# Two-head attention rounds in another order: PE weighs the values of three pairs back first, then scores, then transposes

## The reference

```python
def global_axial_attention(q, k, v, gq, gk):        # "A": 8 heads of 64, 2 key/value heads
    ...
        s = jnp.einsum('bqkgd,bskd->bkgqs', qi, k).astype(jnp.float32)
        p = jax.nn.softmax(s, axis=-1)
        return jnp.einsum('bkgqs,bskd->bqkgd', p.astype(v.dtype), v)
...
def neighbourhood_attention(q, k, v, rpb):           # "C": 8 heads of 64, a window of columns, a bias
    ...
        s = s + bias.astype(jnp.float32)[None]
        p = jax.nn.softmax(s.reshape(B, C_HEADS, GRID_W, win_r * NA_COLS), axis=-1)
        return jnp.einsum('bhqrj,brqjhd->bqhd', p, v_nb)
```

## Time and profile before

| | us |
|---|---|
| median of 3 runs | 3302.02 |
| lowest, highest | 3294.03, 3302.18 |
| the profiled execution | 3301.9 |
| its span, first to last instruction | 3300.1 |
| PE busy in the span | 3174.4 (96%) |
| DVE, ACT, POOL busy | 1688.9, 1196.6, 145.8 |
| mean granted TensorE clock | 0.989 |

### The profile page before, as it was taken

How to read it: one execution, slowest core, us unless ns; L and a number is a source line. 1 busy time by engine, 2 the same in 40 slices (tenths; PEclk the granted TensorE clock), 3 DMA queues, 4 the chain that set the end, 5 groups by cost and what they waited for, 6 DMA issues and landing times.

```text
span 3300.1 us, 42252 instructions
## 1 busy us (share of the span) xinstructions
PE 3174.4 (96%) x17113; PEld 2612.7 (79%) x17113; DVE 1688.9 (51%) x2230; ACT 1196.6 (36%) x1612; POOL 145.8 (4%) x203
## 2 busy tenths in 40 slices
PE   8899999999989899999999889999999999999999
PEld 7667888888867588888887568888888888788887
DVE  3565446553444644565527855552543434555543
ACT  3544235343333622444323244342321222344432
POOL 2030000000011200000002110000000000000000
PEclk9999999999989999999999999999999999999999
DMA  6112323322422032233322113323221121223222
GB/s 170 49 39 77 101 90 102 102 83 97 110 68 74 27 102 91 101 102 97 100 96 78 53 58 102 102 83 108 92 89 64 64 90 64 75 85 101 89 89 89
DMA packets 229781, 285.02 MB, mean 86 GB/s; under 512 B 5156, under 2 KB 188492, under 8 KB 229388
## 3 DMA queue, kind: packets, MB, share of 16 engines
q1 hardware_dynamic: 225628, 266.89, 24.8%
q0 software_dynamic: 4016, 16.16, 2.0%
HBM read 280.93 MB, written 2.10 MB: 86 GB/s over the span
## 4 chain that ended last, share of the span: by engine, by line
PE 87%; DVE 10%; ACT 2%; issue 1%; POOL 0%; DMA 0%; DVEq 0%; POOLq 0%; ACTq 0%
PE ps L1595 19%; PE ps L1597 18%; PE ps L1596 18%; PE ps L1710 6%; PE ps L1709 6%; PE ps L1708 6%; DVE t_wlo L1045 2%; ACT t_whi L674 1%; PE ps L1634 1%; PE ps L1633 1%; PE ps L1632 1%; PE ps L1802 1%; DVE t_vb L1514 1%; PE ps L1981 1%; PE ps L2160 1%
## 5 line engine op out<-in xcount | busy, mean ns | idle before, releaser
L1045 DVE TENSOR_TENSOR t_wlo<-t_wraw,t_whi 128x2048 fp32r<-128x2048 f32 x252 | 583.1, 2314 | 1302.7 <-ACT t_whi L674 1302.7
L1595 PE MATMUL ps<-t_hh,t_whi 128*128 128x512 f32 (+1 forms) x2704 | 1012.0, 374 | 10.8 <-DVE t_accv L1241 5.1
L1596 PE MATMUL ps<-t_hl,t_whi 128*128 128x512 f32 (+1 forms) x2704 | 1002.6, 371 | 0.0
L1597 PE MATMUL ps<-t_hh,t_wlo 128*128 128x512 f32 (+1 forms) x2704 | 1002.5, 371 | 0.0
L674 ACT ACTIVATE t_whi<-t_wraw 128x2048 fp32r<-128x2048 f32 x252 | 482.8, 1916 | 1374.4 <-PE ps L1597 954.0
L1595 PEld LDWEIGHTS ps<-t_hh,t_whi 128*128 128x128 f32 x2704 | 510.6, 189 | 113.2 <-issue 14.9
L1596 PEld LDWEIGHTS ps<-t_hl,t_whi 128*128 128x128 f32 x2704 | 510.6, 189 | 88.3 <-issue 2.4
L1597 PEld LDWEIGHTS ps<-t_hh,t_wlo 128*128 128x128 f32 x2704 | 510.4, 189 | 87.8
L1708 PE MATMUL ps<-t_whi,t_midh 128*128 128x512 f32 x704 | 274.4, 390 | 0.0
L1710 PE MATMUL ps<-t_whi,t_midl 128*128 128x512 f32 x704 | 274.0, 389 | 0.0
L1709 PE MATMUL ps<-t_wlo,t_midh 128*128 128x512 f32 x704 | 273.9, 389 | 0.0
(11 more groups left out here) (275 smaller groups left out, 3749.8 us busy)
## 6 DMA issues: line engine op xcount, KB each, us to landing
t_wraw<-in_w_in_dram SPq DMA_DIRECT2D x46, 1024.0 KB, 5.3
t_wraw<-in_w_up_dram SPq DMA_DIRECT2D x44, 1024.0 KB, 5.1
t_wraw<-in_ffn_w_in_dram SPq DMA_DIRECT2D x44, 1024.0 KB, 5.1
t_wraw<-in_w_kv_dram SPq DMA_DIRECT2D x24, 1024.0 KB, 5.1
t_wraw<-in_w_down_dram SPq DMA_DIRECT2D x20, 1024.0 KB, 5.0
t_wraw<-in_ffn_w_out_dram SPq DMA_DIRECT2D x20, 1024.0 KB, 5.0
t_wraw<-in_w_branch_dram SPq DMA_DIRECT2D x12, 1024.0 KB, 5.0
t_wraw<-in_w_q_dram SPq DMA_DIRECT2D x12, 1024.0 KB, 5.1
```

The costliest lines, as they stand in the source:

```text
L1045: v.tensor_tensor(wlo[slot][:, :], wraw[slot][:, :], whi[slot][:, :].bitcast(F32), ALU.subtract).then_inc(w_lo, 1)
L1595: te.matmul(out, wh, xh, start=first, stop=False)
L1596: te.matmul(out, wh, xl, start=False, stop=False)
L1597: return te.matmul(out, wl, xh, start=False, stop=last)
```

## The change

On all engines the rounds are written in one new order. In round j:

- PE: weigh pair j-3, scores of pair j, (pooling matmul), transposes of both heads of pair j-2. Scores of pair j wait for the exponentials of pair j-2 in A and in C.
- ACT: exponentials of pair j-1, (pooling, `y_round`), copies of both heads of pair j-2.
- DVE: maxima of pair j, divide both heads of pair j-1, (`y_rest`).

Scores of pair 1 now stand ahead of the last `row_tile` of the stage before. In C the maxima write the sums back into the PSUM bank of the scores, and the exponentials read them there, so the wait for `turned` moves from DVE's maxima to ACT's exponentials. `pA` gets a fourth slot. The two tiles at the end are split: one ahead of the last transposes, one behind them, and the last weighing comes after both, in A too. The split of a weight chunk and the pooling steps on ACT and DVE stand in other rounds. In A the banks of the scores are swapped.

```diff
-POOL_PAIRS = (3, 7, 11, 15)
 SLOTS = 3
+PAIR_SLOTS = 4
...
-                pA = sb("pA", SLOTS * T, stack=u)
+                pA = sb("pA", PAIR_SLOTS * T, stack=u)
...
-        def score_bank(n):
-
-            return bank(6 * (n // 2 % 2) + n % 2)
+        def score_bank(kind, n):
+
+            return bank(6 * ((n // 2 + (kind == "A")) % 2) + n % 2)
...
-                slots = 4 if kind == "C" else SLOTS
+                per = 2 if kind == "C" else 4
+                pairs = 4 * per
 
                 def exp(n):
                     g = n0 + n
-                    s, q = g % slots, g % 4
+                    s, q = g % PAIR_SLOTS, g % 4
                     act.wait_ge(maxed, g + 1)
-                    if kind == "A" and n >= slots:
-                        act.wait_ge(turned, g - slots + 1)
+                    if n >= PAIR_SLOTS:
+                        act.wait_ge(turned, g - PAIR_SLOTS + 1)
+                    p, scores = pbuf[:, s * T:(s + 1) * T], score_bank(kind, n)
                     if kind == "C":
                         for i in range(2):
-                            p = pbuf[:, s * T + i * WIN:s * T + (i + 1) * WIN]
-                            ins = sc.activation(p, p, ACT.Exp, bias=small[:, 2 * q + i:2 * q + i + 1], scale=-1.0,
+                            ins = sc.activation(p[:, i * WIN:(i + 1) * WIN], scores[:, i * WIN:(i + 1) * WIN], ACT.Exp,
+                                                bias=small[:, 2 * q + i:2 * q + i + 1], scale=-1.0,
                                                 accum_out=small[:, 8 + 2 * q + i:9 + 2 * q + i])
                     else:
-                        ins = sc.activation(pbuf[:, s * T:(s + 1) * T], score_bank(n), ACT.Exp, bias=small[:, q:q + 1],
-                                            scale=rq[:, n:n + 1], accum_out=small[:, 8 + q:9 + q])
+                        ins = sc.activation(p, scores, ACT.Exp, bias=small[:, q:q + 1], scale=rq[:, n:n + 1],
+                                            accum_out=small[:, 8 + q:9 + q])
                     ins.then_inc(probs, 1)
...
-                exp(0)
-                exp(1)
-                if 0 in extra:
-                    extra[0]()
-                per = 2 if kind == "C" else 4
-                pairs = 4 * per
-                for j in range(pairs + 2):
-                    if 1 <= j <= pairs:
-                        copy(2 * j - 1)
-                    if j > per and (j - 1) % per == 0:
-                        y_round(n0, (j - 1) // per - 1, per, kind)
-                    if j < pairs:
-                        copy(2 * j)
-                    if j < pairs - 1:
-                        exp(2 * j + 2)
-                        exp(2 * j + 3)
-                    if j and j in extra:
+                for j in range(1, pairs + 4):
+                    if j <= pairs:
+                        exp(2 * j - 2)
+                        exp(2 * j - 1)
+                    if j in extra:
                         extra[j]()
+                    if j >= per + 3 and (j - 3) % per == 0:
+                        y_round(n0, (j - 3) // per - 1, per, kind)
+                    if 2 <= j < pairs + 2:
+                        copy(2 * j - 4)
+                        copy(2 * j - 3)
...
-                pair_maxima(n0, 0, scores_in, factors)
-                divide(n0, pbuf, T)
-                for j in range(pairs + 2):
+                for j in range(pairs + 4):
+                    if j in extra:
+                        extra[j]()
                     if j < pairs:
-                        divide(n0 + 2 * j + 1, pbuf, T)
-                    if j == 0:
-                        if j in extra:
-                            extra[j]()
-                        pair_maxima(n0, 1, scores_in, factors)
-                    if j < pairs - 2:
-                        pair_maxima(n0, j + 2, scores_in, factors)
-                    if j < pairs - 1:
-                        divide(n0 + 2 * j + 2, pbuf, T)
-                    if j and j in extra:
-                        extra[j]()
-                    if j > per and (j - 1) % per == 0:
-                        pair_out((j - 1) // per - 1)
+                        pair_maxima(n0, j, scores_in, factors)
+                    if 1 <= j <= pairs:
+                        divide(n0 + 2 * j - 2, pbuf, T)
+                        divide(n0 + 2 * j - 1, pbuf, T)
+                    if j >= per + 3 and (j - 3) % per == 0:
+                        pair_out((j - 3) // per - 1)
...
-                def scores_c(n, s, q, l=l):
+                def scores_c(n, q, l=l):
                     hp, bb = divmod(n // 2, 2)
                     dve.wait_ge(e2_ready, 4 * l + hp + 1)
-                    if n >= 4:
-                        dve.wait_ge(turned, STEPS[f"C{l}"] + n - 3)
                     for i in range(2):
                         at = (2 * (n % 2) + (2 * bb + i) // 3) * WIN
-                        ins = v.tensor_tensor_reduce(pC[:, s * T + i * WIN:s * T + (i + 1) * WIN],
-                                                     score_bank(n)[:, i * WIN:(i + 1) * WIN], e2[hp][:, at:at + WIN], 1.0,
-                                                     -2 * NEG, ALU.add, ALU.min, small[:, 2 * q + i:2 * q + i + 1])
+                        scores = score_bank("C", n)[:, i * WIN:(i + 1) * WIN]
+                        ins = v.tensor_tensor_reduce(scores, scores, e2[hp][:, at:at + WIN], 1.0, -2 * NEG, ALU.add, ALU.min,
+                                                     small[:, 2 * q + i:2 * q + i + 1])
...
-            def pair_attention(kind, n0, scores, pbuf, weigh, v_drained=None, behind=None, extra={}):
+            def pair_attention(kind, n0, scores, pbuf, weigh, behind, extra={}):
 
                 pairs = 8 if kind == "C" else 16
-                scores(1)
-                for j in range(pairs + 1):
+                for j in range(2, pairs + 3):
+                    if j == pairs + 2:
+                        behind(1)
+                    if j >= 3:
+                        pe.wait_ge(pt_ready, n0 + 2 * j - 4)
+                        weigh(j - 3)
                     if j < pairs:
-                        turn_probs(n0, 2 * j, pbuf)
-                    if j < pairs - 2:
-                        pe.wait_ge(probs if kind == "A" else maxed, n0 + 2 * j + 2)
-                        scores(j + 2)
+                        pe.wait_ge(probs, n0 + 2 * j - 2)
+                        scores(j)
                     if j in extra:
                         extra[j]()
-                    if j == pairs and behind:
-                        behind()
-                    if j == 1 and v_drained:
-                        pe.wait_ge(drained, v_drained)
-                    if j:
-                        pe.wait_ge(pt_ready, n0 + 2 * j)
-                        weigh(j - 1)
-                    if j < pairs:
-                        turn_probs(n0, 2 * j + 1, pbuf)
+                    if j == pairs + 1:
+                        behind(0)
+                    if j < pairs + 2:
+                        turn_probs(n0, 2 * j - 4, pbuf)
+                        turn_probs(n0, 2 * j - 3, pbuf)
...
+                    if j == 0:
+                        pe.wait_ge(drained, keys_out)
...
                 scores_c(0)
+                scores_c(1)
...
-                def first_a(c=FIRST[f"a_qkv{l}"], d=DRAINS[f"a_qkv{l}"]):
-                    start(c, d=d)
-                    rows_out(c, (hh, hl), bank0=0).then_inc(w_used, 1)
-
-                pair_attention("C", STEPS[f"C{l}"], scores_c, pC, weigh_c(l), v_drained=2 + d + 6, behind=first_a)
+                def first_a(m, c=FIRST[f"a_qkv{l}"], d=DRAINS[f"a_qkv{l}"]):
+                    if m == 0:
+                        start(c, d=d)
+                    ins = row_tile(c, (hh, hl), m, bank(m))
+                    if m:
+                        ins.then_inc(w_used, 1)
+
+                pair_attention("C", STEPS[f"C{l}"], scores_c, pC, weigh_c(l, 2 + d + 6), first_a)
...
                 scores_a(0)
+                scores_a(1)
...
-                def first_gate(c=c, d=d):
-                    start(c, d=d)
-                    row_tile(c, (hh, hl), 0, bank(6))
-
-                pair_attention("A", STEPS[f"A{l}"], scores_a, pA, weigh_a(l),
-                               behind=first_gate,
-                               extra={j: lambda g=g: pooled_out(g) for g, j in enumerate(POOL_PAIRS)})
-                row_tile(c, (hh, hl), 1, bank(7)).then_inc(w_used, 1)
+                def first_gate(m, c=c, d=d):
+                    if m == 0:
+                        start(c, d=d)
+                    ins = row_tile(c, (hh, hl), m, bank(6 + m))
+                    if m:
+                        ins.then_inc(w_used, 1)
+
+                pair_attention("A", STEPS[f"A{l}"], scores_a, pA, weigh_a(l), first_gate,
+                               {4 * g + 5: lambda g=g: pooled_out(g) for g in range(4)})
                 pe.wait_ge(y_lo, PAIRS[f"A{l}"] + 4)
```

37 lines of the change are left out of this document (19 added, 18 removed).

## The result

The changed kernel takes **3268.7 us** (median of 4 executions, 3267.8 to 3269.4) against 3299.6 for the kernel before (median of 4, 3294.0 to 3302.2). The ratio is 0.9908, 95% interval 0.9891 to 0.9925: 0.9% faster. The forecast was 3274 with 3267 to 3293 around it. The profiled execution has a span of 3265.9 us, 34.2 less than that of before. How large the gain looks depends on which executions of the kernel before stand beside it: over all that were timed for this document they took from 3288.8 to 3303.8 us (see "What the low clock hangs on").

What follows compares the result with a forecast made beforehand. PE, 96% busy, was held in C by a ring through three engines, whose idling also lowered its clock. Gaining 28.5 us in C and losing 0.9 in A takes 3301.9 to 3274 us, range 3267 to 3293.

Steps and rivals of the forecast that it cites:

- -4 and +5 for POOL: Bounds in us on the forecast of 3274, for DVE slowed beside POOL's windows in attention A.
- +3 for the handover: Upper bound on the forecast: the handover from ACT's copy to PE's weighing may add some 3 us.
- The new round: PE's round in C and A: 1.84 until the weighing starts, weighing 1.02, scores 1.06, together 3.92 us.
- C, 39.38 us, gain 28.5: Attention C, old start of pair 1's scores to last weighing's start: 39.38 us per layer; 13.50 + 15.03 gained.
- the ring: Old C round: PE's transposes wait for DVE's divide, behind maxima that wait for PE's transpose to read their pC slot.
- Maxima in PSUM: C's maxima in place in PSUM: taken at 0 extra; upper end doubles 0.42 us each, 1.7 us per round.
- A, 79.44 us: Attention A, old start of pair 1's scores to the end: 0.71 gained in layer 0, 1.66 lost in layer 1.
- The term of 2.0 us for DVE beside POOL: In A, about four rounds beside POOL slow DVE: 0 to 4.4 us, taken as 2.0.
- The wait of 1.44 us behind the last weighing: End of A: a new 1.44 us wait, since the gates need the result out of PSUM, no longer under a tile.
- The rival of the falling clock: PE's clock falls in new rounds, 2.9 us more each; half of 40 rounds gives 3332 us. Chance 0.09.
- The rival of a longer bare wait: ACT still busy when transposes end: 0.3 us more in each of 44 waits, 13 us, 3287 us. Chance 0.14.
- The rival of C as DVE's: Costlier maxima in PSUM make DVE need 4.7 us per C round; 10 us more, 3284 us. Chance 0.07.

Runs made afterwards that it cites:

- e3: Kernel before with one edit: C's maxima write back into PSUM, the exponentials read there, two waits moved; old order kept. Span 3281.8 us.
- e4: Changed kernel with one part undone: C's maxima write to pC in SBUF again, the new order kept. 3271.7 us.
- e2: Kernel before with the new order in attention A alone, C as before. 3286.1 us.
- e12: Kernel before with the new order in attention A alone, the same program profiled a second time. Span 3293.8 us.
- e8: Changed kernel with ACT doing the second copy of each round twice, lengthening PE's idling. 3298.3 us.
- e9: Changed kernel with ACT doing the second copy of each round three times, lengthening PE's idling further. 3383.4 us.

## Why the prediction was right, point by point

The mechanism was right in C, which carries the gain. The total came out 5.3 us under the forecast of 3274, and the bounds that the prediction names do not reach it: -4 and +5 for POOL and +3 for the handover, around 3274, give 3270 to 3282, and not the 3267 to 3284 that it writes. The measured 3268.7 lies 1.3 below 3270. That the stated range holds it is owed to those 3 us, for which no term stands, so in part to luck. What was missing is in A's term and in code that the sum left out, as follows.

- **The new round, 3.92 us.** Measured 3.92 in C and 3.91 in A, with its parts 1.83, 1.03 and 1.06 against 1.84, 1.02 and 1.06. Transposes, copy and handover were taken from rows of the old kernel in which the same instructions stood in another order, and they kept their lengths.
- **C, 39.38 us, gain 28.5.** Measured 39.43 in both layers, gain 28.4. e3 and e4 show that the mechanism was rightly named: cutting the link through `pC` by either part removes DVE's wait for the transpose. What the forecast did not say is that each part would do alone. It also took the old clock as given. Measured against e2, where C before had its full clock, the gain would be 7.5 us per layer: about half of C's gain is the ring, half the clock that went with the ring in five of eight passes. So the time of the changed kernel was forecast from rows that hold, while the gain also hangs on which execution of the kernel before is taken: by medians it is 31.0 us, beside the fastest that was timed (3288.8) 20.1.
- **Maxima in PSUM.** Taken at no cost. They take 0.43 to 0.47 us where they took 0.42, some 0.04 more each, all under DVE's idle time of 0.9 us in a round. The upper bound of twice the length was far off.
- **A, 79.44 us; here a term was mis-sized.** Measured from the same mark (190.04, one group of scores ahead of the 191.10 at which the scores of pair 2 start now) to 267.62: 77.6 us, and as much in layer 1. The term of 2.0 us for DVE beside POOL is the wrong one: the rounds beside POOL cost about 0.5 in all. It was priced from DVE's own work of one round there (5.0 us), but a pair now has two rounds until its transposes, so that DVE can make up in the second what it loses in the first; this reason is read from the order and was not tested by a run. The four pooling matmuls cost 0.96 each (4.88 - 3.92), not 1.06, which is the other 0.4. The wait of 1.44 us behind the last weighing came out at 1.42. So A was no loss of 0.9 us but a gain of 2.8: 2.6 in layer 0 and 0.2 in layer 1. Of that gain 2.4 us are owed to the old A: in layer 0 the clock was 0.81 from 204 to 222 us, where the first rounds lie, and at the same place of layer 1 it was 1.00 (the table's 86.9 beside 84.5). In the second profile of the kernel before it is layer 1 that is longer (84.5 and 86.4). The new A took 84.1 in all eight passes of after, e2, e4 and e12.
- **What was not in the sum.** By the prediction's marks, the stretches between the attentions are 0.7 us shorter, and the code behind the second A 2.4 us, without an edit in it. In kernels that share this code it took from 2147.6 to 2153.8 us, so 2.4 is within what it varies by. Together with A's 3.7 this is the whole distance of the profile from the forecast: 27.6 + 3.7 + 0.7 + 2.4 = 34.4, measured 34.2.
- **The rival of the falling clock** (slower, 0.09). It did not come, and the row of A with 0.62 us of idling at a clock of 1.00 was the right one to lean on. e8 and e9 put numbers to it: no fall at 0.74 and 1.37 us per round, 1.74 mixed, 2.00 a heavy fall. The rule of the Trainium skill, "TensorE: Matmul & The Clock Gate", section "A second HAM failure mode: psum-queue depth-cycling", by which a PE that idles briefly but often can swing between both levels, is borne out at 1.74 and 2.00 us and not at 0.74 or 1.37.
- **The rival of a longer bare wait** (0.14). The rows in front of the weighing say 0.74 us in nearly every round, at most 0.88. ACT was never late.
- **The rival of C as DVE's** (0.07). DVE idles 0.9 us per round of C.

## What to carry to other kernels

When an engine waits for a result that it has just asked for, look for the next independent group of its own work and put it there: the changed order left 0.74 us of latency bare in 44 places, and filling most of them by swapping two blocks of PE's loop took off another 23 us. Before crediting a gain to fewer waits, read the clock on both sides and profile the old kernel twice, since half of the gain in C was clock that the old kernel lost in some passes and not in others. And a wait that two separate edits can each remove should be costed for each alone: e3's is one changed operand of DVE's and two moved waits, and brings most of it.

## What the runs showed of the hardware

- The granted clock of one program is not the same in each execution. With PE idle for 1.74 us in each round of 5.06, C of layer 1 ran at 1.00 in e2 and at 0.79 in e12. With 1.37 us per 4.55 it stayed at 1.00 in all four attentions of e8, with 2.00 it was 0.80 to 0.89 in those of e9.
- A DVE instruction of 2.29 us with two SBUF inputs took 7.3 to 10.1 beside a series of 32 short POOL instructions that took 12.8, or it came through in 2.3 to 2.6 and the series took 14.9. Of 27 such meetings 18 went the first way and 9 the second; one program had both, in different executions.
- DVE's maxima that write to the PSUM bank they read take 0.43 to 0.47 us; to SBUF, 0.42. One of them in the changed kernel:

```profile
104.95 0.47 DVE L1321 CUSTOM_DVE_ANT_0 ps<-ps,t_e 128x256 f32<-128x256 f32 x1
```
